# Attention of eight decode samples in two waves of four on column tiles, with two page-transposing steps moved among the prompt's units

## What is computed

```python
def mla_attend(q_lat, q_rope, ckv, krope, q_pos, k_pos):
    ...
    s = (jnp.einsum('bthc,bsc->bhts', ql, ckv)
         + jnp.einsum('bthr,bsr->bhts', qr, krope)).astype(jnp.float32) * SOFTMAX_SCALE
    s = jnp.where(k_pos[None, :] <= qp[:, None], s, -jnp.inf)
    p = jax.nn.softmax(s, axis=-1).astype(ckv.dtype)
    return jnp.einsum('bhts,bsc->bthc', p, ckv)
```

## Time and profile before

| | |
|---|---|
| median of 3 runs | 2007.27 us (2006.75 to 2009.55) |
| the profiled execution | 2006.67 us |
| its span, first to last instruction | 2005.1 us |
| outside the span | 1.6 us |
| PE busy | 1825.3 us, 91% of the span |
| DVE busy | 1217.3 us, 61% |
| ACT busy | 922.2 us, 46% |
| mean granted TensorE clock | 0.912 of 2.4 GHz |

### The profile page before, as it was taken

The page is one execution under the profiler, slowest core; times in us unless marked ns, Lnnn a source line. Parts: engine busy times, 40 slices in busy tenths (PEclk is TensorE's granted clock), DMA queues, the critical chain, the costliest instruction groups (busy, mean ns, idle before and its releaser), DMA issues.

```text
span 2005.1 us, 23401 instructions
## 1 busy us (share of the span) xinstructions
PE 1825.3 (91%) x8410; PEld 1402.3 (70%) x8410; DVE 1217.3 (61%) x1254; ACT 922.2 (46%) x802; POOL 91.2 (5%) x156
## 2 busy tenths in 40 slices
PE   5998969999979878888699999999999999999993
PEld 3746657999955543347587787877878778787783
DVE  2102684444344332223588888888888888888886
ACT  1100022443201111102377777777777677777774
POOL 2000020001001002200100000000000000000001
PEclk9995569999989568898799999999999999999997
DMA  9640042434724002202399999999999999999993
GB/s 271 237 178 1 0 48 98 163 98 128 222 85 173 8 0 63 69 14 105 125 372 365 356 370 341 387 365 356 368 343 386 359 363 368 345 380 354 374 368 135
DMA packets 220336, 458.37 MB, mean 229 GB/s; under 512 B 11045, under 2 KB 45418, under 8 KB 220282
## 3 DMA queue, kind: packets, MB, share of 16 engines
q1 hardware_dynamic: 209034, 428.96, 59.8%
q0 software_dynamic: 9968, 28.12, 5.0%
q10 hardware_dynamic: 1280, 0.54, 0.2%
HBM read 440.29 MB, written 17.30 MB: 228 GB/s over the span
## 4 chain that ended last, share of the span: by engine, by line
PE 82%; DVE 8%; ACT 5%; issue 3%; DMA 1%; POOL 0%; SPq 0%; POOLq 0%; ACTq 0%; DVEq 0%
PE bank L374 15%; PE bank L376 15%; PE bank L375 15%; PE bank L370 8%; ACT wpart L1542 3%; PE wide L376 2%; PE wide L374 2%; PE wide L375 2%; PE bank L733 2%; DVE wpart L892 2%; PE wide L716 2%; PE bank L774 2%; PE bank L546 1%; PE bank L678 1%; PE wide L848 1%
## 5 line engine op out<-in xcount | busy, mean ns | idle before, releaser
L892 DVE TENSOR_TENSOR wpart<-mring,wpart 128x2048 fp32r<-128x2048 f32 x339 | 775.6, 2290 | 158.3 <-ACT wpart L1542 157.5
L1542 ACT ACTIVATE wpart<-mring 128x2048 fp32r<-128x2048 f32 x336 | 643.1, 1917 | 202.9 <-PE bank L376 109.7
L374 PE MATMUL bank<-wpart,xgp 128*128 128x512 f32 x896 | 361.0, 403 | 6.7 <-DVE wpart L892 5.1
L375 PE MATMUL bank<-wpart,xgp 128*128 128x512 f32 x896 | 354.7, 396 | 0.0
L376 PE MATMUL bank<-wpart,xgp 128*128 128x512 f32 x896 | 354.6, 396 | 0.0
L374 PEld LDWEIGHTS bank<-wpart,xgp 128*128 128x128 f32 x896 | 168.8, 188 | 49.9 <-DVE wpart L892 10.2
L376 PEld LDWEIGHTS bank<-wpart,xgp 128*128 128x128 f32 x896 | 168.7, 188 | 40.9
L375 PEld LDWEIGHTS bank<-wpart,xgp 128*128 128x128 f32 x896 | 169.0, 189 | 37.9
L374 PE MATMUL bank<-ffparts,wpart 128*128 128x288 f32 (+1 forms) x528 | 159.2, 301 | 5.2 <-DVE ffparts L892 4.2
L376 PE MATMUL bank<-ffparts,wpart 128*128 128x288 f32 (+1 forms) x528 | 157.4, 298 | 0.0
L375 PE MATMUL bank<-ffparts,wpart 128*128 128x288 f32 (+1 forms) x528 | 155.1, 294 | 0.0
(11 more groups left out here) (347 smaller groups left out, 2143.7 us busy)
## 6 DMA issues: line engine op xcount, KB each, us to landing
mring<-in_w_gate_m SPq DMA_DIRECT2D x114, 1024.0 KB, 5.3
mring<-in_w_up_m SPq DMA_DIRECT2D x113, 1024.0 KB, 5.7
mring<-in_w_down_m SPq DMA_DIRECT2D x112, 1024.0 KB, 5.3
ring<-in_w_in_a SPq DMA_DIRECT2D x6, 2048.0 KB, 24.3
ring<-in_w_down_d SPq DMA_DIRECT2D x8, 1344.0 KB, 7.1
ring<-in_w_gate_d SPq DMA_DIRECT2D x5, 2048.0 KB, 9.0
ring<-in_w_up_d SPq DMA_DIRECT2D x5, 2048.0 KB, 7.9
xs<-arena POOLq DMA_DIRECT2D x4, 1664.0 KB, 17.3
```

The lines of the kernel that those rows point to most:

```text
L374: pe.matmul(o, a[0], b[0], start=start, stop=False)
L375: pe.matmul(o, a[1], b[0], start=False, stop=False)
L892: return v.tensor_tensor(dst, src, high.bitcast(F32), ALU.subtract)
L1542: a.activation(wpart[:, stage(h), 0, :], mring[:, place(h % IH), :], ACT.Copy).then_inc(S["hi_ready"], 1)
```

## The change

The samples go in two waves of four. A wave's four samples stand on partitions 0 to 31, 32 to 63, 64 to 95 and 96 to 127 of the outputs, so that each of their matmuls writes another column tile of the array. A wave's 1024 keys are taken in four steps of 256 keys: a step turns 2 pages of each of the four samples (again 24 transposes in 6 groups, with copies on ACT and DVE) into one of two buffers, and its scores are 12 products of 256 columns. Softmax, turning of the probabilities (now 9 transposes of 128 columns), scaling and turning of the output are done once per wave on 128 partitions. ACT copies half of the turned probabilities.

Steps are software-pipelined: the transposes of step t + 2 stand between the scores of t and t + 1. Steps 0 and 1 stand after units 9 and 12 of the prompt, on PE, DVE and ACT alike.

All 8 samples get a page buffer of their own, laid over ring slots 0 to 4, so SP's page loads move from `dd4` and the end of its chunks to one block before `wo1`, each sample behind the chunk that its buffer lies over. Expert halves 1 to 4 then wait for the first wave's product, and `wo1` and half 0 for the second's. POOL's rotary loads move in the same way.

```diff
-BUFS = 3
+WAVES, WB = 2, 4
+QK = 256
+STEPS = PAST // QK
+TGROUPS = 6
+EARLY = [9, 12]
...
+        PTS = area(16320, NPG + 1, WB * TS)
+        turnT = [area(at, CT + 1, WB, QK) for at in (10176, 13248)]
...
+        nat = ring[:, 0:5, :].rearrange("p s n -> p (s n)").rearrange("p (k n) -> p k n", k=NB)
+        pagebuf = [nat[:, k, :] for k in (2, 3, 4, 5, 0, 1, 6, 7)]
+        under_page = ["dkv", "dq", "uk", "uk", "uq0", "uq0", "uq1", "uq1"]
...
+            def cache_transposes(t):
+                w, qd = divmod(t, STEPS)
+                for g in range(TGROUPS):
...
+                    for bb in range(2):
+                        b = w * WB + pair * 2 + bb
+                        for pg in range(2):
+                            page = qd * 2 + pg
...
+                            ins = pe.transpose(bank[n % 2][0:rows, (bb * 2 + pg) * P:(bb * 2 + pg + 1) * P], src, ident)
+                    ins.then_inc(S["tp_full"], 1)
+
+            def s_scores(t):
+                w, qd = divmod(t, STEPS)
+                pe.wait_ge(S["tpa_free"], 3 * (t + 1))
+                pe.wait_ge(S["tpd_free"], 3 * (t + 1))
...
+                kv = turnT[t % 2]
+                for k in range(CT):
+                    for b in range(WB):
+                        pe.matmul(wide[b * TS:(b + 1) * TS, qd * QK:(qd + 1) * QK], qls[:, k, w * WB + b, :], kv[:, k, b, :],
+                                  start=(k == 0), stop=False)
+                for b in range(WB):
+                    ins = pe.matmul(wide[b * TS:(b + 1) * TS, qd * QK:(qd + 1) * QK], qrs[:, w * WB + b, :], kv[0:ROPE, CT, b, :],
+                                    start=False, stop=True)
+                ins.then_inc(S["part_done"], 1)
...
+            def s_attend(w):
...
+                for pg in range(NPG + 1):
+                    for b in range(WB):
+                        kv = ctk[w * WB + b][:, pg, :] if pg < NPG else ctok[0:TS, 2, 0:CKV]
+                        rows = P if pg < NPG else TS
+                        ins = pe.matmul(bank[3][b * TS:(b + 1) * TS, 0:CKV], PTS[0:rows, pg, b * TS:(b + 1) * TS], kv,
+                                        start=(pg == 0), stop=(pg == NPG))
+                ins.then_inc(S["av_full"], 1)
...
             for u in range(len(units)):
                 p_attend(u)
...
+                if u in EARLY:
+                    cache_transposes(EARLY.index(u))
             pe.wait_ge(S["ol_ready"], NU)
...
+            s_scores(0)
+            cache_transposes(2)
+            s_scores(1)
+            cache_transposes(3)
+            s_scores(2)
+            cache_transposes(4)
+            s_scores(3)
+            cache_transposes(5)
+            s_probs(0)
+            s_scores(4)
+            s_attend(0)
+            cache_transposes(6)
+            s_scores(5)
+            s_turn(0)
+            cache_transposes(7)
+            s_scores(6)
+            s_scores(7)
+            s_probs(1)
+            s_attend(1)
+            s_turn(1)
...
+            for t in range(2, 5):
+                cache_evac(t)
+            sample_max(0)
+            cache_evac(5)
+            probs_evac(0)
...
-                if name == "dd4":
...
+                if name == "wo1":
+                    sp.wait_ge(S["ld_pages"], 16)
+                    for b in range(NB):
+                        sp.wait_ge(*release[CH[under_page[b]]])
+                        load_cache(b)
+                    sp.wait_ge(S["av_full"], 1)
+                    for h in range(1, 5):
+                        expert_half(0, h)
+                    sp.wait_ge(S["av_full"], 2)
```

More of the change, by code:

```diff
@@ L234, in build @@
         S = {n: sem(n) for n in names}
-        ck_full = [sem(f"ck_full{k}") for k in range(BUFS)]
-        cr_full = [sem(f"cr_full{k}") for k in range(BUFS)]
+        ck_full = [sem(f"ck_full{b}") for b in range(NB)]
+        cr_full = [sem(f"cr_full{b}") for b in range(NB)]
         w_full = [sem(f"w_full{k}") for k in range(SLOTS)]
@@ L682, in _, with s_turn @@
+            def s_turn(w):
+                pe.wait_ge(S["os_ready"], w + 1)
+                for k in range(CT):
+                    ins = pe.transpose(bank[2][:, k * P:(k + 1) * P], osb[:, k * P:(k + 1) * P], ident)
+                ins.then_inc(S["ol_full"], 1)
             p_scores(0)
@@ L685, in _ @@
                 p_attend(u)
[L687 to L735, removed]
@@ L1177, in prompt_max, with cache_evac @@
                 softmax_max(u, bank[5 + u % 2][:, 0:(q + 1) * P], P, q * P, c("pmask"))
+            def cache_evac(t):
+                if t >= 2:
+                    v.wait_ge(S["part_done"], t - 1)
+                for g in (1, 3, 5):
+                    v.wait_ge(S["tp_full"], TGROUPS * t + g + 1)
+                    part, pair = divmod(g, 2)
+                    rows = P if part < CT else ROPE
+                    v.tensor_copy(turnT[t % 2][0:rows, part, 2 * pair:2 * pair + 2, :],
+                                  bank[1][0:rows, :].rearrange("p (b n) -> p b n", b=2)).then_inc(S["tpd_free"], 1)
             prompt_max(0)
@@ L1191, in _ @@
                               bank[4][:, 0:CT * P].rearrange("p (a b) -> p a b", a=CT)).then_inc(S["ol_ready"], 1)
+                if u in EARLY:
+                    cache_evac(EARLY.index(u))
             NU = len(units)
[L1194 to L1225, removed]
@@ L1495, in _, with cache_evac @@
             units = [(h, q) for h in range(H) for q in range(2)]
+            def cache_evac(t):
+                if t >= 2:
+                    a.wait_ge(S["part_done"], t - 1)
+                for g in (0, 2, 4):
+                    a.wait_ge(S["tp_full"], TGROUPS * t + g + 1)
+                    part, pair = divmod(g, 2)
+                    rows = P if part < CT else ROPE
+                    a.activation(turnT[t % 2][0:rows, part, 2 * pair:2 * pair + 2, :],
+                                 bank[0][0:rows, :].rearrange("p (b n) -> p b n", b=2), ACT.Copy).then_inc(S["tpa_free"], 1)
             for u, (h, q) in enumerate(units):
@@ L1702, in expert_half @@
                              src.rearrange("e (c p) n -> p (e c) n", p=P)).then_inc(half_full[place(h)], 16)
+            for n, (name, parts) in enumerate(chunks):
+                if name == "wo1":
[7 more added lines that the diff above has]
+                    sp.wait_ge(S["av_full"], 2)
+                if slot_of[n] >= 4 and n >= SLOTS:
+                    sp.wait_ge(S["gd_full"], GD_CKV)
+                elif n >= SLOTS:
+                    sp.wait_ge(*release[behind[n]])
+                for k, w, at, rows, src in parts:
+                    dst = ring[0:rows, slot_of[n], at:at + k * w].rearrange("p (c n) -> p c n", c=k)
+                    sp.dma_start(dst, src).then_inc(w_full[slot_of[n]], 16)
             def item_rest(it, e):
@@ L1716, in item_first @@
                     expert_half(e, h)
-            under = [CH[name] for name in ("dkv", "dkv", "dq", "dq", "uk", "wo1", "wo1")]
-            for h in range(HALVES):
-                if h == 5:
-                    for b in range(2, NB):
-                        if b == 2:
-                            sp.wait_ge(*release[CH["uq1"]])
-                        else:
-                            sp.wait_ge(S["av_full"], b - BUFS + 1)
-                        load_cache(b)
-                sp.wait_ge(*release[under[h]])
-                expert_half(0, h)
+            expert_half(0, 0)
+            sp.wait_ge(*release[CH["wo1"]])
+            expert_half(0, 5)
+            expert_half(0, 6)
             with sp.Fori(0, E - 1) as it:
@@ L1774, in shape_constants @@
     }
-    x = np.arange((2 * NB - 1) * NS)
-    parts["smask"] = np.where((x[None, :] // NS == NB - 1) & (x[None, :] % NS <= r[:, None] % NS), 0.0, NEG)
+    parts["smask"] = np.concatenate([np.where((t[None, :] // NS == w * WB + r[:, None] // TS)
+                                              & (t[None, :] % NS <= r[:, None] % NS), 0.0, NEG) for w in range(WAVES)], axis=1)
     half = ROPE // 2
```

159 lines of the change are left out of this document (90 added, 69 removed).

## The result

The changed kernel takes 1892.0 us (median of four runs, 1889.7 to 1897.2) against 2007.9 before: ratio 0.9426, 95% interval [0.9405, 0.9447]. The profiled executions, which the rest goes by, took 2006.67 and 1891.04 us: 115.6 us to account for, where the sum had 88.2.

A forecast was written before the change was run, and what follows sets the result against it. It took PE's own time and waits to bound the kernel. From 2006.7 us, -98.5 (samples' stage), +11.4 (early steps) and -1.1 (queues) gave 1918.5, with the median 0.6 higher: 1919 us, range 1901 to 1930.

The forecast's parts named there:

- Parts 1 to 3: Samples' stage: four column tiles overlapping, transposes in pipelined steps, and their summed time, 62.3 us against 160.8, saving 98.5.
- step 5: Samples' stage: the transpose step standing behind the first wave's maximum and exp on DVE and ACT, 6.5 us.
- the lower clock: Samples' stage: the clock stays at the lower level all along, 85 us instead of 62.3, total 1942; chance 0.12.
- two tiles: Samples' scores and products: only two column tiles work at a time, +19.5 us, total 1938; chance 0.08.
- one tile: Samples' scores and products: column tiles work one at a time, stage 115 us, total about 1972; chance 0.09.
- the emptied array: Samples' matmuls: every change of tile empties the array, 192 changes costing 52 us, total 2024; chance 0.04.
- Part 4: Prompt's attention: two early transpose steps hide under nothing and cost 5.7 us each, 11.4 for both.
- The lower bound: Prompt's attention: the early steps cost nothing if a higher clock after them gives all their time back.
- Part 5: DMA queues: SP loses its page issues before `dd4`, winning 1.1 us; later page and weight loads keep nobody waiting.
- the Sum: Whole kernel: samples' stage -98.5, early steps +11.4, queues -1.1, together -88.2 us from the profiled 2006.7, so 1918.5.

The follow-up runs named there:

- the loop exchange: Changed kernel with its attend's two loops exchanged, so one sample's nine products, all on one column tile, are issued before the next sample's: 1919.2 us, ratio 0.9552.

## Why the prediction was right or wrong

**Right: what bounded it, and the samples' stage (Parts 1 to 3).** 60.3 against 62.3 forecast. The terms for the scores, one regular step and the first product were met within 0.15 us each, step 5 took 7.2 us (755.09 to 762.33) in place of 6.5, and 0.8 of the 2 us are the clock's: the share of 0.88 in place of 0.86 gives 61.5 in the same formula. That tiles overlap was taken from L527, two tiles; four do so as well, at 3.96 times one. The rivals of the lower clock, of two tiles, one tile and the emptied array thus fall, and the loop exchange shows what one tile at a time costs in the waves' products alone: a samples' stage of 86.6 us, 26.3 more. By the Trainium skill (TensorE: Matmul & The Clock Gate, Measured speedup vs the span model), three tiles gave 2.38 and four would have given an estimated 3.2; the measured 3.96 decides here.

**Mis-sized: Part 4.** Each early step was to cost 5.7 because "the trace shows the prompt's units at the lower level throughout". In the profiled execution both cost 7.5 where they stand, not 11.4, since they ran at the full clock for most of their length, and 5.1 came back from the units behind them, +2.5 in all; over eight traces it was 0 to 4.7. The lower bound (a higher clock gives all of it back) had named the mechanism; I chose the other end, from a trace without such steps. The Trainium skill (TensorE: Matmul & The Clock Gate, Part 4: PE-mode transpose) has no full clock in transposes; the rise at 706.4, within a step of transposes, disagrees.

**Part 5, the stall before `dd4`.** It went: the residual additions now come every 9.18 us, without the longer pair of the earlier trace rows. Two of them, from the changed kernel:

```profile
506.42 0.45 DVE L1110 TENSOR_TENSOR xT<-xT,bank 128x288 f32<-128x288 f32 x1 [1.33 <-PE bank L382]
...
515.60 0.46 DVE L1110 TENSOR_TENSOR xT<-xT,bank 128x288 f32<-128x288 f32 x1 [1.34 <-PE bank L382]
```

But the regular distance was 9.12, and the dense layer as a whole is not shorter (in the rows on `ffparts` above, its first and last start are 215.8 us apart before and 216.4 after). The longer pitch of its matmuls, an estimated 1.7 us, took away more than the 1.1 that the stall had cost; the forecast had no term for that either. The page issues ended at 682.3 and not at 666, still before the first early step at 704.2. None of PE's waits in the samples' stage ends with a DMA, so no page and no weight came late.

**The step that failed: the Sum.** It held three terms and left every other stretch as it was. The diff shows `smask` growing by four columns, and I costed that edit at nothing, without a word on what lies behind it in SBUF. It is worth 18.9 us in this pair of executions, and the kernel before with this effect alone takes 0.9909 of its time. With both operands back at a slow distance, the change takes 1912.5 us: inside the range, and 6.5 below the forecast, which Part 4's error more than covers. None of my rivals had an effect outside the samples, so the range ended at the best case of the parts I had costed (1901), 9 us above the result.

The forecast's parts and the operands' distance account for it together: 0.9909 x 0.9527 = 0.944, against 0.9426 measured.

No kernel tried here beats the changed one: its operands already lie at a fast distance, and the place of the early steps makes no difference that can be told.

## What to carry to other kernels

- A longer constant moves every tensor allocated behind it. Where a loop of long matmuls is bound by PE, look at where its two operands lie before and after an edit, and try a few spacers of 32 to 256 bytes: here one of 32 bytes alone was worth 0.9% in the old kernel. Look at every loop: the edit that made the experts' matmuls shorter came with slightly longer ones in the dense layer.
- To put small matmuls on column tiles is half of it; they must also alternate between tiles in the order of issue, product by product.
- Extra work on PE in a stretch at the lower clock may cost less than its length, since it can raise the clock for what follows. Price it at both levels, say which work behind it would gain, and look at several traces: here the same two steps cost nothing in some and 4.7 us in one.

## What the runs showed of the hardware that was not expected

- A 512-column matmul of the experts starts 227 ns after the one before when stationary and moving operand lie a multiple of 256 bytes apart in their partitions, and 232 to 234 ns at the distances 32, 64, 128 and 224 modulo 256. The loop's code is the same in all. In the dense layer, with 288 columns and the roles exchanged, the matmuls became 1.1 ns longer with the change (132.2 to 133.3 ns); whether by the distance is open.
- Four column tiles of 32 give 3.96 times the pace of one for 256-column products at full clock (4.16 against 16.46 us).
- The granted clock rose to 1.00 within an early step of transposes, and was there while units of the prompt's attention ran (716.6 to 730.3 in the changed kernel, 708.1 to 732.0 in the one with everything 32 bytes up); the same units without the steps stayed at the lower level.
